# Hyena stage of a two-block network: six hand-placed side tasks move back by one weight chunk

## The reference, cut to what matters

```python
z = depthwise_conv(u @ w_in + b_in, w_short, b_short)   # w_in is 1024 x 3072, short filter of 3 taps
x0, x1, v = jnp.split(z, 3, axis=-1)
h_fwd, h_bwd = hyena_filters(...)                       # 256 taps for each of 1024 channels
v = v * x1
v = two_sided_fft_conv(v, h_fwd, h_bwd) + v * d_bias
return (v * x0) @ w_out + b_out
```

## Time and profile before

| | us |
|---|---|
| median of 3 runs | 1739.28 |
| lowest and highest run | 1736.54 and 1741.97 |
| the profiled execution, its own time | 1741.85 |
| its span in the trace | 1740.1 |
| PE busy in the span | 1642.2 (94%) |
| DVE busy | 1137.5 (65%) |
| ACT busy | 763.0 (44%) |
| mean granted clock of TensorE | 0.971 of full speed |

### The profile page before, as it was taken

The page is one execution under the profiler, slowest core; times in us unless marked ns, Lnnn a source line. Parts: engine busy times, 40 slices in busy tenths (PEclk is TensorE's granted clock), DMA queues, the critical chain, the costliest instruction groups (busy, mean ns, idle before and its releaser), DMA issues.

```text
span 1740.1 us, 29309 instructions
## 1 busy us (share of the span) xinstructions
PE 1642.2 (94%) x12199; PEld 1516.4 (87%) x12199; DVE 1137.5 (65%) x1558; ACT 763.0 (44%) x888; POOL 11.5 (1%) x25
## 2 busy tenths in 40 slices
PE   6999789999999889999999999999989999999997
PEld 3899667899998776899998999988989999999996
DVE  6966773577678657555557346666555665878786
ACT  2422253355333332456433235544433333767664
POOL 0000000000000000000001000000000000000000
PEclk9899799999999999999999899999998999999999
DMA  8444430266686422234567244422332444778783
GB/s 332 173 170 153 161 121 25 97 225 241 240 306 216 162 97 73 76 133 178 194 224 253 107 161 170 146 95 100 146 127 97 176 166 183 281 299 308 298 307 115
DMA packets 43512, 310.23 MB, mean 178 GB/s; under 512 B 5239, under 2 KB 5624, under 8 KB 6984
## 3 DMA queue, kind: packets, MB, share of 16 engines
q1 hardware_dynamic: 41760, 301.75, 47.3%
q0 software_dynamic: 1248, 5.72, 1.0%
q10 hardware_dynamic: 392, 1.12, 0.2%
HBM read 307.53 MB, written 1.05 MB: 177 GB/s over the span
## 4 chain that ended last, share of the span: by engine, by line
PE 78%; DVE 14%; ACT 4%; issue 2%; DMA 1%; ACTq 0%; SPq 0%; DVEq 0%
PE ps L632 16%; PE ps L634 15%; PE ps L633 15%; PE ps L638 4%; PE ps L640 4%; PE ps L639 4%; DVE macc L1921 3%; DVE wlo L1909 3%; ACT whi L1424 2%; PE ps L689 1%; PE ps L690 1%; PE ps L691 1%; PE ps L1289 1%; PE ps L1363 1%; PE ps L849 1%
## 5 line engine op out<-in xcount | busy, mean ns | idle before, releaser
L1909 DVE TENSOR_TENSOR wlo<-raw,whi 128x2048 fp32r<-128x2048 f32 x218 | 497.8, 2288 | 291.0 <-ACT whi L1424 290.6
L632 PE MATMUL ps<-uhi,whi 128*128 128x256 f32 x1728 | 502.1, 291 | 13.5 <-DVE ulo L1951 4.2
L1424 ACT ACTIVATE whi<-raw 128x2048 fp32r<-128x2048 f32 x218 | 415.9, 1910 | 200.0 <-PE ps L634 143.1
L634 PE MATMUL ps<-ulo,whi 128*128 128x256 f32 x1728 | 494.3, 286 | 0.0
L633 PE MATMUL ps<-uhi,wlo 128*128 128x256 f32 x1728 | 494.3, 286 | 0.0
L632 PEld LDWEIGHTS ps<-uhi,whi 128*128 128x128 f32 x1728 | 337.3, 195 | 23.0 <-issue 16.6
L633 PEld LDWEIGHTS ps<-uhi,wlo 128*128 128x128 f32 x1728 | 337.3, 195 | 1.1 <-issue 1.0
L634 PEld LDWEIGHTS ps<-ulo,whi 128*128 128x128 f32 x1728 | 336.8, 195 | 0.0
L632 PE MATMUL ps<-hid_hi,whi 128*128 128x256 f32 x512 | 145.2, 284 | 1.6 <-ACTq L1608 1.6
L634 PE MATMUL ps<-hid_lo,whi 128*128 128x256 f32 x512 | 144.0, 281 | 0.0
L633 PE MATMUL ps<-hid_hi,wlo 128*128 128x256 f32 x512 | 143.9, 281 | 0.0
(11 more groups left out here) (466 smaller groups left out, 2810.0 us busy)
## 6 DMA issues: line engine op xcount, KB each, us to landing
raw<-weights_in SPq DMA_DIRECT2D x258, 1024.0 KB, 4.8
y<-weights_in SPq DMA_DIRECT2D x18, 1024.0 KB, 5.3
mstart<-mod_start_in SPq DMA_DIRECT2D x4, 2048.0 KB, 19.7
w1c<-cmp_w_in POOLq DMA_DIRECT2D x1, 2048.0 KB, 13.0
h<-x_in SPq DMA_DIRECT2D x1, 1024.0 KB, 7.8
ctx<-ctx_in SPq DMA_DIRECT2D x1, 1024.0 KB, 18.6
y<-decay_in ACTq DMA_DIRECT2D x1, 1024.0 KB, 4.8
out<-y SPq DMA_DIRECT2D x4, 256.0 KB, 2.2
```

The source lines that it names most:

```text
L632: mm(o, w0, x0, start=first, stop=False, **kw)
L634: return mm(o, w0, x1, start=False, stop=last, **kw)
L1424: fn(whi[:, sl, :], raw_at(i) if n is None else raw[:, sl, :], ACT.Copy).then_inc(s("hi_ready"), 1)
L1909: tt(wlo[:, sl, :], raw_at(i) if n is None else raw[:, sl, :], f32(whi[:, sl, :]), ALU.subtract).then_inc(s("lo_ready"), 1)
```

## The change

Nothing is added or removed; six pairs of tasks move to another slot. On PE, the transforms of the first half go from slots 4 and 5 to 5 and 6, the taps of the second half from 5 and 6 to 6 and 7, the transposes of `v` from 7 and 9 to 8 and 10, and the transforms of the second half from 8 and 9 to 9 and 10. On ACT the first half's stores go from 5 and 6 to 6 and 7; the second half's stores both go to slot 10, one ahead of the copies of the transposes and one behind them. On DVE `taps_of(1, ...)` goes from slots 6 and 7 to 7 and 8. The first half's taps stay where they were on PE (1 and 2) and on DVE (2 and 3).

```diff
--- before.py
+++ after.py
@@ -973,15 +973,15 @@
 
                 if g in (1, 2):
                     filter_taps(0, g - 1)
-                if g in (4, 5):
-                    filter_spec(0, g - 4)
                 if g in (5, 6):
-                    filter_taps(1, g - 5)
-                if g in (7, 9):
+                    filter_spec(0, g - 5)
+                if g in (6, 7):
+                    filter_taps(1, g - 6)
+                if g in (8, 10):
+                    turn_v(g - 8)
                     turn_v(g - 7)
-                    turn_v(g - 6)
-                if g in (8, 9):
-                    filter_spec(1, g - 8)
+                if g in (9, 10):
+                    filter_spec(1, g - 9)
 
             pe.wait_ge(s("vtok_stored"), 4)
             for half in range(2):
@@ -1651,13 +1651,15 @@
                     ins = fn(zpad[:, g % 2, m, 1:T + 1], ps[:, g % 2, m * T:(m + 1) * T], ACT.Identity, bias=pcol("hy_b_in", first + m, 1))
                 ins.then_inc(s("hy_drained"), 1)
                 split(I_HY + g + RING)
-                if g in (5, 6):
-                    store_spec(0, g - 5)
-                if g in (9, 10):
-                    store_spec(1, g - 9)
+                if g in (6, 7):
+                    store_spec(0, g - 6)
+                if g == 10:
+                    store_spec(1, 0)
                 if g in (8, 10):
                     turned(g - 8)
                     turned(g - 7)
+                if g == 10:
+                    store_spec(1, 1)
             for half in range(2):
                 a = slice(4 * half, 4 * half + 4)
                 act.wait_ge(*nth("hy", "normed", half + 1))
@@ -2221,8 +2223,8 @@
                 short_conv(g)
                 if g in (2, 3):
                     taps_of(0, g - 2)
-                if g in (6, 7):
-                    taps_of(1, g - 6)
+                if g in (7, 8):
+                    taps_of(1, g - 7)
             gate_of(6, pcol("mix_post", 8, 8), 1, 2)
             scale_of(3, pcol("mlp_pre", 8, 8), 1, 4)
             dve.wait_ge(s("spec_stored"), 4)
```

## The result

| | before | changed |
|---|---|---|
| median, us | 1741.97 (11 runs, 1736.54 to 1745.46) | 1732.59 (9 runs, 1728.65 to 1736.44) |
| ratio, 95% interval | | 0.9949 [0.9935, 0.9963] |
| the profiled execution, its own time, us | 1741.85 | 1729.87 |
| its span, us | 1740.1 | 1728.0 |

Two further executions of the changed kernel took 3187 us, at a granted clock of 1.0; the cause isn't known, and they are left out. The ratio stands for 8.9 us less (6.4 to 11.3). The forecast was 8.1 less, a ratio of 0.9953, and 1731.2 us in a range of 1726.5 to 1736.5. So the kernel became faster by about what was forecast, and the time was within the range. The kernel before, timed anew beside it, has a median 2.7 us above the 1739.28 that the forecast started from, so the ratio is the fairer comparison.

What follows compares the result with a forecast made beforehand. PE, busy 94% of the span, was taken as the bound, losing time in two waits for taps and the half clock behind them. Gains of 7.52 + 0.56 = 8.08, taken as 8.1, bring 1739.28 to 1731.2 us, range 1726.5 to 1736.5.

Steps and rivals of the forecast that it cites:

- What bounds the stage: Hyena stage: PE waits twice for DVE's taps, 9.0 us in total, each wait followed by a transform at half clock.
- The first gap: PE's wait ahead of the first transform: 4.60 us gone plus 2.92 from full clock, 7.52 us gained.
- The margin: First half's taps ready at 598.75, PE wants them after chunk 5 at 599.90: 1.15 us to spare.
- The second gap: PE's wait ahead of the third transform: stays, shrinking from 4.63 to 4.07 us, 0.56 us gained.
- The half clock behind it: Third transform, after the remaining wait: clock falls again, 5.72 us as before; bounds 3.53 and 7.06.
- a draw: Clock gate runs on its own clock, so the 2.92 us lost after the first wait may vary between runs.
- Rival 1: Clock's share not there to be won; only the waits come back, 5.2 us, giving 1734.1; chance 0.15.
- What moves at no cost: ACT's four copies in slot 10, other stores, transposes and DMA: no delay, 4.2 us of cover before chunk 11's drain.
- Behind the products: From the complex products to the end: everything follows what went before, so the 8.1 us are carried through.
- (2): Wait ahead of the third transform no longer lowers the clock: 10.3 us gained, giving 1729.0; chance 0.13.
- (3): Wait only moved: DVE late to slot 7, gain handed to the later wait, time stays 1739.3; chance 0.08.
- (4): Half clock outlasts the third transform, to the end of chunk 11: 17.3 us, giving 1748.5; chance 0.03.

Runs made afterwards that it cites:

- e2: Kernel before, own order, with nine unread matmuls on PE ahead of the first and of the third transform; ratio 0.9978, stage 110.66 us.
- e3: Changed kernel with the third transform moved to PE's slot 10, ahead of the fourth, and ACT's two stores behind the transposes' copies; ratio 0.9911, stage 101.15 us.
- e6: Kernel before with two PE tasks moved: first transform from slot 4 to 5, third from slot 8 to 9; ratio 0.9928, stage 101.18 us.
- e1: Kernel before with one task moved: the first transform from PE's slot 4 to 5, ahead of the second; ratio 0.9959, stage 108.20 us.
- e4: Changed kernel with the transposes of v put back into PE's slots 7 and 9; ratio 0.9977, stage 111.10 us.
- e8: Changed kernel with transposes in PE's slots 7 and 9, and ACT's second first-half store ahead of the split in slot 7; ratio 0.9969, stage 107.80 us.
- e5: Changed kernel, own order, with eight unread matmuls on PE ahead of the third transform; ratio 0.9945, stage 105.24 us.

## Why the prediction was right

**What bounds the stage.** Right. The two waits of line 745 were on the path, and each also brought half clock. e2 shows the clock's part alone (4.96 us in the stage for the two), e3 and e6 the removal of both waits with their falls.

**The first gap** (forecast 4.60 + 2.92 = 7.52). e1, which does nothing else, shortened the stage by 7.42. In the changed kernel the first transform begins at 595.83, when chunk 5 ends, and takes 3.53 us. The margin was as forecast (1.15): the last operation of the taps ends at 593.92 + 0.69 = 594.61, 1.2 us before.

```profile
593.92 0.69 DVE L2212 TENSOR_TENSOR sq<-sq 128x512 f32<-128x512 f32 x1
```

**The second gap** (forecast to shrink from 4.63 to 4.07). It measured 3.89. The reason given, one chunk between taps and transform, held: e3 and e6 put a second one between and the gap was gone. The wait was described with too few ends, though. I tied it to chunk 7 through DVE's backlog; e4 showed that chunk 8 comes within 0.29 us of deciding it. The forecast's own numbers held this: chunk 8 ends at 628.15, and 2.85 us of drain and split give 631.00, against the 631.34 at which DVE comes to it.

**The half clock behind it** (forecast 5.72, bounds 3.53 and 7.06). It fell again, and the transform took 6.24, 0.52 more. This is the term that was mis-sized. The smaller gap gave 0.18 back: 8.08 - 0.52 + 0.18 = 7.74, against 7.82 measured in the stage. In the five profiles that have this wait (before, changed, e1, e4, e8) the chain gives the third transform 5.76, 6.28, 5.94, 6.43 and 6.23 us. So the price of a fall is no constant, and it stayed within the forecast's bounds. That it is a draw, as the prediction weighed, isn't shown: these are five programs with one profile each, and the work ahead of the wait differs between them. Rival 1, by which the first fall costs little in the timed executions, would give 5.2 us less; the interval of 6.4 to 11.3 excludes that.

**What moves at no cost.** Right. ACT's four copies in slot 10 end before chunk 11 does:

```profile
649.38 1.02 ACT L1630 ACTIVATE spec<-ps 128x1024 f32<-128x1024 f32 x1
650.28 1.09 ACT L1635 ACTIVATE vtok<-ps 128x512 f32<-128x512 f32 x2
651.24 1.06 ACT L1630 ACTIVATE spec<-ps 128x1024 f32<-128x1024 f32 x1
656.90 0.84 ACT L1651 ACTIVATE zpad<-ps,par 128x256 f32<-128x256 f32 x2 [4.61 <-PE ps L634]
```

The last store ends at 652.30 and the next drain starts at 656.90, 4.6 us later (4.2 forecast).

**Behind the products.** 1063.5 and 1063.3 us, as forecast. That they agree to 0.2 us is luck in part, for the ten profiles have 1059.7 to 1066.8 there. What bears out that the stage's gain is carried to the end are the times: 8.9 us less for 7.8 in the stage here, 15.5 for 14.5 in e3. The products start at 664.66 and not at about 668.5, because the stage began 4.08 us earlier; with that added it is 668.7.

**The rivals.** The clock's share was there (rival 1), the second gap did lower the clock (2), the first wait was not handed to the second gap (3), and the half clock ended with the third transform (4): the fourth took 3.44 at 647.68. The part of the 8.9 us of the ratio beyond 7.8 lies inside its interval and has no place in the profile.

## What to carry to other kernels

When PE waits for a side task that another engine does behind its main work, count how many units of main work lie between the producer's slot and the consumer's. Here one chunk (5.75 us) was too few for a chain of 10.3 us (from 588.47, the end of chunk 3, to the taps at 598.75: drain, two splits, convolution, taps) and two were enough; moving both ends of the pair together, as this change did for the second half, leaves the wait nearly as it was (4.6 and 3.9 us). Price such a wait with the half clock behind it, and then look for the fewest moves: two on one engine shortened the stage by 14.4 us, the change's six pairs by 7.8.

## What the runs showed of the hardware

A wait of 1.82 us was enough to lower TensorE's clock (e4: 0.57 in the stretch that follows, 0.84 over chunk 8), while one of 3.07 us left it at 1.00. Ahead of the short wait PE had run at 1.00 with the raw taps last; in e8 the same raw taps without the wait left the clock at 1.00. The length of a wait alone therefore doesn't tell whether the clock falls. The Trainium skill, "TensorE: Matmul & The Clock Gate", section "HAM oscillation — how this bites in real kernels", describes falls of the clock behind PE's waits for DMA. The waits here are for another engine's arithmetic, and behind those of 3.8 to 4.6 us the trace agrees: granted clock 0.54 to 0.63 in the transform that follows.

The same instructions ahead of the stage took 556.86 to 568.08 us in ten profiles, a spread larger than the effect under study. Of the 11.2 us between the shortest (the changed kernel) and the longest (e5), 9.2 are PE's busy time over the same instructions, 503.8 against 513.0 us, at a mean granted clock of 0.97 against 0.95.
